# Gated feed-forward stages: one 512-column product for both parts of h, the halves of the bank added by two engines

## The reference

```python
def swiglu(h, w_gate, w_up, w_down):
    return (jax.nn.silu(h @ w_gate) * (h @ w_up)) @ w_down

h = modulate(x, norm_pre[l, 0], mod[:, 0, 0], mod[:, 0, 1])
x = residual_add(x, swiglu(h, ffn_w_gate[l, 0], ffn_w_up[l, 0], ffn_w_down[l, 0]), norm_post[l, 0], mod[:, 0, 2], 0.5)
```

## Time and profile before

| | us |
|---|---|
| median of 3 runs | 1729.32 |
| lowest, highest | 1728.82, 1733.48 |
| the profiled execution, its time | 1728.25 |
| the profiled execution, its span | 1726.5 |
| one gated stage from its third chunk on, four such | 112.0 |
| one down stage of 11 chunks | 57.2 to 59.9 |

### The profile page before, as it was taken

One profiled execution on the slowest core, in us unless ns is written; L12 is line 12 of the kernel. 1 busy time (PEld: TensorE's weight loads), 2 busy tenths in 40 slices (PEclk: granted clock), 3 DMA queues, 4 the chain that ended last, 5 costly groups with the idle time before them and its releaser, 6 DMA issues.

```text
span 1726.5 us, 29665 instructions
## 1 busy us (share of the span) xinstructions
PE 1670.9 (97%) x12368; PEld 1555.2 (90%) x12368; DVE 1259.0 (73%) x1815; ACT 877.2 (51%) x1241; POOL 21.9 (1%) x39
## 2 busy tenths in 40 slices
PE   3999999998999999999999999999999999999998
PEld 3999989987999889989989997999889989989996
DVE  7777879987777666676878775778666676878553
ACT  4555466654544365665463435543365665463432
POOL 0000000000000000000000000000000000000000
PEclk9999999999999999999999999999999999999999
DMA  9879746786677944746548786677745846547552
GB/s 385 327 255 257 258 165 223 197 311 268 244 279 277 291 169 181 225 156 232 205 149 294 283 231 240 241 277 279 292 165 181 224 162 230 201 150 263 193 171 112
DMA packets 71077, 398.92 MB, mean 231 GB/s; under 512 B 8224, under 2 KB 8736, under 8 KB 36256
## 3 DMA queue, kind: packets, MB, share of 16 engines
q1 hardware_dynamic: 67968, 387.56, 63.9%
q0 software_dynamic: 2976, 9.47, 1.6%
HBM read 395.92 MB, written 1.08 MB: 230 GB/s over the span
## 4 chain that ended last, share of the span: by engine, by line
PE 84%; DVE 5%; ACT 4%; DVEq 2%; DMA 2%; issue 1%; ACTq 1%; SPq 1%
PE att L649 18%; PE lin L472 18%; PE lin L473 18%; PE lin L474 18%; PE att L752 2%; DVE lo L1284 2%; ACT hi L901 2%; PE lin L512 2%; PE lin L514 2%; PE lin L522 1%; PE att L804 1%; DVEq L1639 1%; DMA ada_s<-in_ada 1%; PE pt L781 1%; DMA ada_w<-in_ada 1%
## 5 line engine op out<-in xcount | busy, mean ns | idle before, releaser
L1284 DVE TENSOR_TENSOR lo<-raw,hi 128x2048 fp32r<-128x2048 f32 x262 | 600.1, 2291 | 278.6 <-ACT hi L901 278.0
L472 PE MATMUL lin<-h_hi,hi 128*128 128x256 f32 x2448 | 689.6, 282 | 3.6 <-DVE ra L1540 2.6
L473 PE MATMUL lin<-h_lo,hi 128*128 128x256 f32 x2448 | 683.3, 279 | 0.0
L474 PE MATMUL lin<-h_hi,lo 128*128 128x256 f32 x2448 | 683.2, 279 | 0.0
L901 ACT ACTIVATE hi<-raw 128x2048 fp32r<-128x2048 f32 x262 | 500.6, 1911 | 190.6 <-PE att L649 116.9
L472 PEld LDWEIGHTS lin<-h_hi,hi 128*128 128x128 f32 x2448 | 460.1, 188 | 7.3 <-issue 7.2
L473 PEld LDWEIGHTS lin<-h_lo,hi 128*128 128x128 f32 x2448 | 460.2, 188 | 1.5 <-issue 1.4
L474 PEld LDWEIGHTS lin<-h_hi,lo 128*128 128x128 f32 x2448 | 460.1, 188 | 0.0
L1300 DVE CUSTOM_DVE_ANT_0 ada_w<-ada_w,cs 128x1024 f32<-128x1024 f32 x179 | 217.8, 1219 | 14.8 <-DMA ada_w<-in_ada 14.7
L1137 ACT ACTIVATE work<-lin 128x256 f32<-128x256 f32 x88 | 33.9, 386 | 280.0 <-PE lin L474 271.8
L649 PE MATMUL att<-hi,act_lo 128*128 128x512 f32 x440 | 135.5, 389 | 0.0
(11 more groups left out here) (299 smaller groups left out, 2061.2 us busy)
## 6 DMA issues: line engine op xcount, KB each, us to landing
raw<-in_w SPq DMA_DIRECT2D x269, 1024.0 KB, 4.9
ada_w<-in_ada SPq DMA_DIRECT2D x179, 512.0 KB, 5.3
ada_s<-in_ada SPq DMA_DIRECT2D x13, 512.0 KB, 15.2
bias<-in_bias POOLq DMA_DIRECT2D x16, 256.0 KB, 4.2
ffn_row<-rows POOLq DMA_DIRECT2D x5, 512.0 KB, 9.6
x<-in_x SPq DMA_DIRECT2D x1, 1024.0 KB, 9.7
dcon<-in_dcon SPq DMA_DIRECT2D x1, 1024.0 KB, 7.6
ra<-rows POOLq DMA_DIRECT2D x2, 512.0 KB, 5.3
```

The costliest lines, as they stand in the source:

```text
L472: mm(out, w_hi, a_hi, start=start, stop=False, skip_group_check=skip)
L473: mm(out, w_hi, a_lo, start=False, stop=False, skip_group_check=skip)
L474: return mm(out, w_lo, a_hi, start=False, stop=stop, skip_group_check=skip)
L1284: tt(lo[c % SPLIT][:], raw[:, c % RAW, :], hi[c % SPLIT][:].bitcast(F32), ALU.subtract).then_inc(*s_lo.up(c))
```

## The change

In the chunks k = 2 to 21 of the four gated stages, the product of the weights' hi part with h's hi part and the one with h's lo part become one product of 512 columns. Its moving operand is a view of two pieces of 256 columns, which lie a fixed distance apart (`H_APART`), so the two parts of h are now one tensor. The product with the weights' lo part stays, with 256 columns. So a chunk has 16 products of 512 columns and 16 of 256, and two banks: bank j holds in its first half what came with h's hi part and in its second half what came with h's lo part. Even chunks take two banks of `att`, odd ones the two of `lin`.

The halves have to be added. ScalarE copies the second halves of both banks to `work` (`gate_half`), VectorE adds the first halves to them (two additions in `swiglu`), and then ScalarE makes silu of the sum. VectorE multiplies after it has made the lo part of chunk k + 3. The down stage now waits for the bank of k = 20 as well. In the gated stages h is kept at the shifted place (`m_hi`, `m_lo`) also for `fm_first`, and some small tensors move in the memory.

```diff
+            def both(stage, k):
+                c = AT[f"{stage}.{k}"]
+                eng.wait_ge(*s_lo.at(c))
+                for before in ((0, 1) if k == 3 else (k - 2,) if k > 3 else ()):
+                    eng.wait_ge(*s_taken_v.at((AT[f"{stage}.{before}"], 0)))
+                out = both_banks(k)
+                s = c % SPLIT
+                for j in range(2):
+                    for t in range(KT):
+                        b = slice((j * KT + t) * P, (j * KT + t + 1) * P)
+                        mm(out[:, j, :], hi[s][:, b], both_parts(t), start=t == 0, stop=False, skip_group_check=True)
+                        ins = mm(out[:, j, 0:SEQ], lo[s][:, b], m_hi[:, t, :], start=False, stop=t == KT - 1,
+                                 skip_group_check=True)
+                ins.then_inc(*s_mm.up((c, 0), c))
...
             def silu_gate(stage, k):
                 c = AT[f"{stage}.{k}"]
                 eng.wait_ge(*s_mm.at((c, 0)))
-                act(work[2 + k % 2][:, 0:SEQ], lin[:, BANK[(c, 0)], 0:SEQ], ACT.Silu).then_inc(*s_gated.up((stage, k)))
+                w = work[2 + k % 2]
+                if k < 2:
+                    act(w[:, 0:SEQ], lin[:, BANK[(c, 0)], 0:SEQ], ACT.Silu).then_inc(*s_gated.up((stage, k)))
+                else:
+                    eng.wait_ge(*s_gate_sum.at((stage, k)))
+                    act(w[:, 0:SEQ], work[k % 2][:, 0:SEQ], ACT.Silu).then_inc(*s_gated.up((stage, k)))
+
+            def gate_half(stage, k):
+                c = AT[f"{stage}.{k}"]
+                eng.wait_ge(*s_mm.at((c, 0)))
+                for j in range(2):
+                    ins = act(work[k % 2][:, j * SEQ:(j + 1) * SEQ], both_banks(k)[:, j, SEQ:2 * SEQ], ACT.Copy)
+                ins.then_inc(*s_halves.up((stage, k)))
...
                 for k in range(FT):
+                    if k > 1:
+                        gate_half(l + ".up0", k)
                     silu_gate(l + ".up0", k)
                     split(AT[f"{l}.up0.{k}"] + SPLIT)
...
             def swiglu(stage, to, k):
                 c = AT[f"{stage}.{k}"]
                 w = work[2 + k % 2]
-                eng.wait_ge(*s_gated.at((stage, k)))
-                tt(w[:, SEQ:2 * SEQ], w[:, 0:SEQ], lin[:, BANK[(c, 0)], SEQ:2 * SEQ], ALU.mult).then_inc(
-                    *s_taken_v.up((c, 0)))
+                if k < 2:
+                    eng.wait_ge(*s_gated.at((stage, k)))
+                    tt(w[:, SEQ:2 * SEQ], w[:, 0:SEQ], lin[:, BANK[(c, 0)], SEQ:2 * SEQ], ALU.mult).then_inc(
+                        *s_taken_v.up((c, 0)))
+                else:
+                    u, banks = work[k % 2], both_banks(k)
+                    eng.wait_ge(*s_halves.at((stage, k)))
+                    tt(u[:, 0:SEQ], banks[:, 0, 0:SEQ], u[:, 0:SEQ], ALU.add).then_inc(*s_gate_sum.up((stage, k)))
+                    tt(u[:, SEQ:2 * SEQ], banks[:, 1, 0:SEQ], u[:, SEQ:2 * SEQ], ALU.add).then_inc(
+                        *s_taken_v.up((c, 0)))
+                    ve.drain()
                 split(c + SPLIT)
+                if k > 1:
+                    eng.wait_ge(*s_gated.at((stage, k)))
+                    tt(w[:, SEQ:2 * SEQ], w[:, 0:SEQ], u[:, SEQ:2 * SEQ], ALU.mult)
                 ve.drain()
                 second_of(k, to, w[:, SEQ:2 * SEQ])
                 ada(c)
```

More of the change, by code:

```diff
@@ L35 @@
 HALF = CH // 2
-BR_SHIFT = 72
 IN_STEP = 56
+H_APART = KT * SEQ + P
 QKV = ["q0", "k0", "v0", "q1", "k1", "v1"]
@@ L79 @@
 UNITS = [(c, part) for c, n in enumerate(NAMES) for part in range(units_of(n))]
+BOTH = [f"{l}.up{s}.{k}" for l in range(LAYERS) for s in (0, 2) for k in range(2, FT)]
 WIDE = (AT["o.up.2"], 0)
-TURNS = [u for u in UNITS if u != WIDE]
+TURNS = [u for u in UNITS if u != WIDE and NAMES[u[0]] not in BOTH]
 BANK = {u: i % 2 for i, u in enumerate(TURNS)}
@@ L177, in program @@
         x = sb("x", [P, 2, D])
-        sb("h_shift", [P, 72])
-        h_parts = [sb("h_hi", [P, KT * SEQ + IN_STEP], F32R)]
+        gain = sb("gain", [P, 2 * 8 + LAYERS * 24])
+        eps = sb("eps", [P, 1])
+        h_all = sb("h", [P, 2 * H_APART], F32R)
+        h_parts = [h_all[:, at:at + KT * SEQ + IN_STEP] for at in (0, H_APART)]
         ada_out = sb("ada_out", [P, ADA_ALL])
-        eps = sb("eps", [P, 1])
-        h_parts.append(sb("h_lo", [P, KT * SEQ + IN_STEP], F32R))
         sb("work_shift", [P, 16])
@@ L193, in program @@
         mod = ada_out
-        gain = sb("gain", [P, 2 * 8 + LAYERS * 24])
         post_gain = sb("post_gain", [P, LAYERS * 24])
@@ L205, in program @@
         with ExitStack() as scope:
+            sb("act_shift", [P, IN_STEP], F32, scope)
             act_hi = sb("act_hi", [P, FT, SEQ], F32R, scope)
@@ L277, in program @@
         s_glu = signal("glu")
+        s_gate_sum, s_halves = signal("gate_sum"), signal("halves")
         s_act, s_taps, s_merged, s_rot, s_lat = (signal("act_made"), signal("taps"), signal("merged"), signal("rot"),
@@ L315, in values_of, with both_parts @@
             return m_v if kind == "mla" else qkv_of(l, kind)[2]
+        def both_parts(t):
+            at = IN_STEP + t * SEQ
+            return h_all[:, 0:2 * H_APART].rearrange("p (a n) -> p a n", a=2)[:, :, at:at + SEQ]
         def by_token(ap):
@@ L367, in across, with both_banks, stage_h @@
             return turned_at[t // 2][:, t % 2 * SEQ:(t % 2 + 1) * SEQ]
+        def both_banks(k):
+            return att[:, 2:4, :] if k % 2 == 0 else lin[:]
+        def stage_h(tag):
+            return (m_hi, m_lo) if tag[2:] in ("pre0", "pre2") else (h_hi, h_lo)
         def bank_of(unit):
@@ L500, in fm_first @@
                 outs = []
+                h1, h2 = stage_h(tag)
                 for i, name in enumerate(names):
@@ L511, in fm_first @@
                             o = out[:, j * SEQ:(j + 1) * SEQ]
-                            mm(o, hi[c % SPLIT][:, b], h_hi[:, t, :], start=t == 0 and j == 0, stop=False,
+                            mm(o, hi[c % SPLIT][:, b], h1[:, t, :], start=t == 0 and j == 0, stop=False,
                                skip_group_check=True)
-                            mm(o, lo[c % SPLIT][:, b], h_hi[:, t, :], start=False, stop=False, skip_group_check=True)
+                            mm(o, lo[c % SPLIT][:, b], h1[:, t, :], start=False, stop=False, skip_group_check=True)
                 for i, name in enumerate(names):
@@ L521, in fm_first @@
                             b = slice((j * KT + t) * P, (j * KT + t + 1) * P)
-                            ins = mm(outs[i][:, j * SEQ:(j + 1) * SEQ], hi[c % SPLIT][:, b], h_lo[:, t, :], start=False,
+                            ins = mm(outs[i][:, j * SEQ:(j + 1) * SEQ], hi[c % SPLIT][:, b], h2[:, t, :], start=False,
                                      stop=t == 3, skip_group_check=True)
@@ L681, in ready @@
                 def ready(t):
+                    if t == 0 and stage[0] != "o":
+                        eng.wait_ge(*s_taken_v.at((AT[f"{stage.replace('down', 'up')}.{FT - 2}"], 0)))
                     eng.wait_ge(*s_act.at((stage, t)))
@@ L870, in _ @@
                 for k in range(2, FT):
-                    fm(f"{l}.up0.{k}")
+                    both(f"{l}.up0", k)
                 down(l + ".down0")
@@ L885, in _ @@
                 for k in range(2, FT):
-                    fm(f"{l}.up2.{k}")
+                    both(f"{l}.up2", k)
                 down(l + ".down2")
@@ L983, in from_x @@
                                scale=gain[:, g + t:g + t + 1])
+                h1, _ = stage_h(tag)
                 for t in (0, 1):
-                    from_x(h_hi[:, t, :], t).then_inc(*s_h_hi.up((tag, t)))
+                    from_x(h1[:, t, :], t).then_inc(*s_h_hi.up((tag, t)))
                 for t in (6, 7):
@@ L992, in h_first @@
                         eng.wait_ge(*s_scaled.at((tag, t)))
-                    act(h_hi[:, t, :], turned_tile(t), ACT.Copy).then_inc(*s_h_hi.up((tag, t)))
+                    act(h1[:, t, :], turned_tile(t), ACT.Copy).then_inc(*s_h_hi.up((tag, t)))
                 for t in (0, 1, 2, 3):
@@ L1261, in _ @@
                 for k in range(FT):
+                    if k > 1:
+                        gate_half(l + ".up2", k)
                     silu_gate(l + ".up2", k)
@@ L1379, in from_x @@
                               ALU.mult, ALU.add)
+                h1, h2 = stage_h(tag)
                 for t in (2, 3):
-                    from_x(h_hi[:, t, :], t).then_inc(*s_h_hi_v.up((tag, t)))
+                    from_x(h1[:, t, :], t).then_inc(*s_h_hi_v.up((tag, t)))
                 for t in (4, 5):
@@ L1389, in modulated @@
                         eng.wait_ge(*s_h_hi.at((tag, t)))
[L1390 removed]
+                    tt(h2[:, t, :], turned_tile(t), h1[:, t, :].bitcast(F32), ALU.subtract).then_inc(
                         *s_h.up((tag, t)))
```

3 lines of the change are left out of this document (1 added, 2 removed).

## The result

| | before | after |
|---|---|---|
| median | 1731.4 us (4 runs, 1728.8 to 1733.9) | 1835.76 us (4 runs, 1834.9 to 1838.2) |
| ratio | | 1.0605, 95% interval 1.0583 to 1.0628 |
| span of the profiled execution | 1726.5 us | 1834.0 us |
| mean granted clock | 0.996 | 0.996 |

The account below looks back on a forecast made before the run. TensorE was taken to bound the kernel before, a closed circle of waits between ScalarE and VectorE after; 3 x 28.9 + 15.2 = 101.8 us on 1728.25 gave 1830, range 1810 to 1850.

Parts of the forecast that it names:

- The links: Gated chunks: successive steps on VectorE and ScalarE from one first addition to the next, each timed start to start.
- turn: Gated stages: one pass through the links, one per chunk, 7.30 us with an `ada` row and 6.16 without.
- The sum: First the links added to 7.30 us; later the stages' delays, 3 x 28.9 + 15.2 = 101.8 us.
- the fifth link: VectorE in a gated chunk: multiplication and drain, 0.42 and 0.10, together 0.52 us.
- The term of 8.3 us: TensorE in gated stages: a chunk takes 5.50 us, 0.10 less, 8.3 us over 80 chunks; hidden, so not added.
- third rival (the circle does not bind): Gated stages: hi part does not wait for the addition, or a turn is under 5.50 us; 1720 us, chance 6%.
- the circle: Gated stages: silu waits for VectorE's addition, hi part stands behind silu, VectorE waits for hi part; 7.30 us, chance 86%.
- The clock: Rival, gated stages: TensorE's clock falls as it idles; half the 76 turns at half clock give 1971 us, chance 3%.
- The two-piece product: Rival, TensorE in gated stages: the 512-column product is not overlapped, 0.389 us each, 1891 us in all, chance 2%.
- The rival of the open circle: The same as the third rival: the circle does not bind, 1720 us, chance 6%.
- The signs to look for: Changed profile, gated stages: about 7.3 us a chunk, silu waiting some 4 us, lo part 1.8, products 0.227 and 0.117 apart.
- 0.8 us after the next turn begins: TensorE in gated stages: its new wait for the bank of two chunks before ends then, with over 1.7 us to spare.

Follow-up runs that it names:

- Experiment 3: The changed kernel with ScalarE's hi part of chunk k + 3 made after the two copies and before silu, from k = 2 on: 1734.1 us, ratio 1.0018.
- experiment 1: The kernel before with one wait more: ScalarE makes the hi part of chunk k + 3 only after VectorE's multiplication of chunk k: 1784.9 us, ratio 1.0311.
- experiment 4: As Experiment 3, with h of the gated stages 56 words lower, where it was before the change: 1725.3 us, ratio 0.9969; timed again 1725.6 us, ratio 0.9975.
- experiment 5: As experiment 4, with the 512-column product taken back into two of 256 columns: 1728.1 us, ratio 0.9991.
- experiment 2: The changed kernel with the 512-column product taken back into two of 256 columns: 1837.8 us, ratio 1.0616.

## Why the prediction was right

Forecast 1830, range 1810 to 1850; measured 1835.8, and against the medians of before measured with it +104.4 us where +101.8 was forecast. By its own steps:

**The bound before and where it went.** TensorE was full and the helpers fitted in. The step that carried everything was the order on ScalarE, with the hi part behind the wait for the addition and VectorE behind the hi part. Experiment 3 undoes this alone and experiment 1 does it alone; together they show it.

**The links.** Forecast and measured, from the timeline of one turn: addition and hand-off 0.46, 0.52; silu 0.31, 0.32; hi part 1.94, 1.93; lo part 2.22, 2.21; multiplication and drain 0.52, 0.49; copy and subtraction 0.71, 0.71; `ada` 1.14, 1.15. The sum was 7.30 and is 7.33, in the mean over 18 turns 131.86 / 18 = 7.33. Without an `ada` row 6.16 was forecast. In the last stage two first additions are 1722.56 - 1716.38 = 6.18 apart:

```profile
1716.38 0.42 DVE L1678 TENSOR_TENSOR work<-att,work 128x256 f32<-128x256 f32 x1
...
1722.56 0.42 DVE L1678 TENSOR_TENSOR work<-lin,work 128x256 f32<-128x256 f32 x1
```

The one link that missed by more than 0.03 is the first: silu began 0.10 after the addition's end, where 0.04 was taken from another pair. What makes this hand-off longer was not tried. The sum came so close partly because that miss of 0.06 and the 0.03 too much in the fifth link stood against each other.

**The sum.** The chain shows when the third chunk of each down stage could start (the last line is that of a whole down stage):

```profile
594.06 46.55 PE att L682 x204
...
1303.37 46.55 PE att L682 x204
...
1767.00 60.10 PE att L682 x264
```

In the first stage 594.1 was forecast and 594.06 came. That is partly luck: the stage itself began 1.1 us earlier in this trace (its first product at 429.82, before at 430.94), and its own lengthening was larger than forecast by as much. From a gated stage's first product to the third chunk of its down stage, the three full stages took 134.3 us each before and 164.2, 164.0 and 164.3 after: 29.9, 29.7 and 29.9 more, where 28.9 was forecast. The last stage added 16.9 before its down stage (1767.00 - 1626.64 against 1659.68 - 1536.23), where 15.2 was forecast. These stages thus hold 4.6 us that the sum lacked: 0.03 a turn make 2.3, and the place of h in the chunks of `fm_first`, which I priced at zero with bounds of 2 us either way, makes 1.2 (11.47 us in place of 11.17 from their first to their last start, as in experiments 3 and 4). The last 1.1 is not accounted for. The delay before the last down stage is 1767.00 - 1659.68 = 107.3. That is the 106.4 of the four stages, less the 1.1 of the earlier start, and 2.0 that came outside them.

**The down stages** gave nothing back, as the sum assumed: 46.55 us for 204 products are 0.228 each, against 0.2268. The second one lost 0.9 us more. TensorE came to its seventh chunk and had to wait until 1104.24 us, because a chunk of raw weights took 12.73 us from its issue to its landing:

```profile
1087.18 12.73 DMA raw<-in_w
```

In the down stages of the kernel before, single loads took up to 14.1 us and TensorE waited for none; the prediction weighed the loads of the gated stages alone. What made this one late for TensorE was not tried.

**TensorE's part** was mis-sized. The term of 8.3 us took the down stage's 0.2268 for the wide product. As the change placed h, a chunk takes 5.65 us and not 5.50: a loss of 4 us against the kernel before. At the better place it is 5.55, half of the gain forecast. It did not touch the sum, because that term was not added. In the forecast's third rival (the circle does not bind) it would have put 1720 where experiment 3 has 1734. The pace of the 512-column product that I took from the down stage did not carry over to an alternation of wide and narrow products: at the better place a pair takes 0.3466 us and not 0.3435. And the place of h, which I had priced only for the first two chunks, costs 0.10 us a chunk in all the others. It turns a gain against the kernel before into a loss, although at either place the wide product beats the two that it replaces. Why an alternation takes longer was not tried.

Of the Trainium skill's rule in "TensorE: Matmul & The Clock Gate", part 2, that the next weights load while the current product runs, experiments 4 and 5 give the measured counterpart: 16 weight loads and product starts fewer are worth 0.05 us a chunk, 3 ns each. So the loads are very nearly hidden, as the page has it. The Trainium skill's same part gives a fixed cost of some 2.5 ns for each product; by it, as an estimate, 16 starts fewer would make 0.04 us a chunk. At the unshifted place 0.05 was measured, at the changed kernel's place 0.10.

**The rivals.** The clock stayed at 1.00 in all stretches, with TensorE busy for 81 to 94% of them. The two-piece product is not even measurably different from one piece. The rival of the open circle named what opens it, a hi part that does not wait for the addition, and this did not hold in the changed kernel.

**The signs to look for** came, three of them a little off. The lo part waits 2.0 us a turn, where 1.8 was forecast. TensorE is idle for 1.5 us a turn, where 1.8 was forecast. Its products take longer, 5.65 us a chunk and not 5.50: the wide one has 0.236 us to the next, where 0.227 was forecast. Its idle time ends with the second addition, as the term "0.8 us after the next turn begins" said (464.41 to 465.31 in the trace, 0.9).

## What to carry to other kernels

When a result now needs two engines in turn (copy, add, activate), look at what stands behind each wait in the in-order queue of the waiting engine, and follow it until it either ends or comes back: if it comes back, the sum of the links is the pace, whatever the load of each engine is. Work that another engine needs and that does not depend on the wait, here the next weights' hi part, goes ahead of the wait; two exchanged lines were worth 102 us here. And a gain on the engine that bounds a stage can only be judged after its helpers' circle is shorter than its own chunk: until then neither a good nor a bad product can be seen.

## What was not expected of the hardware

The place in SBUF of the moving operand of a product changes the pace of the products. Counted in words modulo 64, the weights' parts start at 24 by the order of the tensors in the program (the traces show no addresses). With h at 24 as well, a chunk of 16 wide and 16 narrow products takes 5.65 us, at 32 and at 0 it takes 5.55, with the same instructions. It is no matter of the wide product: products of 256 columns alone start 0.120 us apart with h at 24 (experiment 2) and 0.1167 with h at 32 (experiment 5). Two pieces of 256 columns 2176 words apart and 512 columns in a row took the same 5.55 us. The down stage has wide products alone, at 0.2268 us each, and there weights and activation both start at 24, without an evident loss. So the coincidence is not a rule for all products; whether the down stage would gain from another place was not tried.
